# 64 instead of 32 tokens scored by gathers and dots, in a fused attention and expert block

## The reference

```python
def peer(h, w_query, sub_keys, expert_u, expert_v):
    qry = (h @ w_query).reshape(B, S, PEER_HEADS, 2, PEER_HALF)      # 8 heads
    sc = jnp.einsum('bshpd,hpnd->bshpn', qry, sub_keys)              # 2 x 128 key scores
    top_s, top_i = lax.top_k(sc, K)                                  # K = 16
    cand = top_s[..., 0, :, None] + top_s[..., 1, None, :]
    best, flat = lax.top_k(cand.reshape(B, S, PEER_HEADS, K * K), K)
    i1 = flat // K
    i2 = flat % K
    experts = (jnp.take_along_axis(top_i[..., 0, :], i1, axis=-1) * PEER_NKEYS
               + jnp.take_along_axis(top_i[..., 1, :], i2, axis=-1)) # of 16384
    g = jax.nn.softmax(best.astype(jnp.float32), axis=-1).astype(h.dtype)
    ...
    act = jax.nn.gelu(jnp.einsum('td,tkd->tk', xt, u), approximate=False) * gt
    return jnp.einsum('tk,tkd->td', act, expert_v[et])
```

## Time and profile before

| what | value |
| --- | --- |
| median of 3 runs | 1690.3 us (1689.53 to 1692.21) |
| the profiled execution, its time | 1693.6 us |
| its span | 1691.7 us |
| PE busy | 1639.4 us, 97% |
| DVE busy | 1370.9 us, 81% |
| ACT, POOL busy | 773.5 us, 782.3 us (46% each) |
| DMA | 432.17 MB, 255 GB/s on the mean |

### The profile page before, as it was taken

The page is one execution under the profiler, slowest core; times in us unless marked ns, Lnnn a source line. Parts: engine busy times, 40 slices in busy tenths (PEclk is TensorE's granted clock), DMA queues, the critical chain, the costliest instruction groups (busy, mean ns, idle before and its releaser), DMA issues.

```text
span 1691.7 us, 24231 instructions
## 1 busy us (share of the span) xinstructions
PE 1639.4 (97%) x8700; PEld 1440.1 (85%) x8700; DVE 1370.9 (81%) x2691; ACT 773.5 (46%) x1327; POOL 782.3 (46%) x441
## 2 busy tenths in 40 slices
PE   6999999999999999999999899999999999999998
PEld 4687877878799999899999889999999978888886
DVE  7457656676688787999999589888879999888887
ACT  3356546543553444576767333333333343333334
POOL 0322222325356665666666355555545654333331
PEclk9999999999999999999999999999999999999999
DMA  8322242334043432668888999999998999999992
GB/s 338 110 100 87 105 181 89 137 124 150 27 142 121 151 129 97 209 235 350 329 334 339 357 390 374 343 367 353 348 363 322 347 400 398 398 367 376 379 357 98
DMA packets 141676, 432.17 MB, mean 255 GB/s; under 512 B 13584, under 2 KB 58640, under 8 KB 135696
## 3 DMA queue, kind: packets, MB, share of 16 engines
q1 hardware_dynamic: 88592, 265.61, 42.6%
q0 software_dynamic: 41472, 151.01, 23.8%
q10 hardware_dynamic: 11520, 14.42, 2.3%
HBM read 389.31 MB, written 41.68 MB: 255 GB/s over the span
## 4 chain that ended last, share of the span: by engine, by line
PE 66%; DVE 25%; DMA 4%; issue 3%; POOL 1%; ACT 1%; SPq 0%; DVEq 0%; ACTq 0%
PE bank L990 29%; PE bank L934 11%; PE bank L709 10%; PE bank L873 4%; DVE rows L1625 4%; DVE hot_j L1751 3%; DVE hot_i L1743 3%; DMA u_raw<-euT 2%; DVE hot_j L1746 2%; PE bank L735 1%; DVE arena L1703 1%; PE bank L796 1%; DVE slots L1636 1%; DVE arena L1661 1%; DVE arena L1653 1%
## 5 line engine op out<-in xcount | busy, mean ns | idle before, releaser
L934 PE MATMUL bank<-h_split,u_split 128*128 128x352 f32 x3072 | 518.3, 325 | 8.8 <-DVE u_split L1619 7.1
L934 PEld LDWEIGHTS bank<-h_split,u_split 128*128 128x128 f32 x3072 | 496.6, 189 | 16.7 <-DVE u_split L1619 8.2
L990 PE MATMUL bank<-v_late,a_late 128*128 128x512 f32 x1440 | 326.7, 389 | 1.6 <-DVE a_late L1797 1.6
L990 PEld LDWEIGHTS bank<-v_late,a_late 128*128 128x128 f32 x1440 | 270.2, 188 | 57.9 <-issue 1.8
L609 POOL DMA_INDIRECT rows<-ev,idx x128 | 175.5, 1371 | 220.8 <-DVE row_sum L1734 194.7
L582 POOL TENSOR_TENSOR block_split<-arena,block_split 128x1024 fp32r<-128x1024 f32 x48 | 118.1, 2465 | 304.7 <-ACT block_split L1054 304.7
L609 POOL DMA_INDIRECT rows<-eu,idx x128 | 187.6, 1466 | 149.6 <-DVE dots L1625 125.1
L592 POOL TENSOR_TENSOR u_split<-u_raw,u_split 128x1024 fp32r<-128x1024 f32 x72 | 173.8, 2417 | 169.7 <-ACT u_split L1199 169.5
L990 PE MATMUL bank<-v_split,a_split 128*128 128x512 f32 x864 | 205.4, 392 | 2.2 <-DVE a_split L1797 2.2
L990 PEld LDWEIGHTS bank<-v_split,a_split 128*128 128x128 f32 x864 | 162.1, 189 | 33.1 <-issue 2.5
L1734 DVE SCALAR_TENSOR_TENSOR row_sum<-rows,agate,row_sum 128x1024 f32<-128x1024 f32 x127 | 162.7, 1281 | 5.7 <-DMA rows<-ev,idx 1.6
(11 more groups left out here) (283 smaller groups left out, 2521.5 us busy)
## 6 DMA issues: line engine op xcount, KB each, us to landing
u_raw<-euT SPq DMA_DIRECT2D x128, 512.0 KB, 8.4
v_raw<-ev SPq DMA_DIRECT2D x128, 512.0 KB, 7.2
arena<-w_blocks SPq DMA_DIRECT2D x50, 512.0 KB, 9.2
arena<-w_ada SPq DMA_DIRECT2D x12, 2048.0 KB, 8.4
gates_scratch<-stage SPq DMA_DIRECT2D x24, 1024.0 KB, 13.6
gates<-gates_scratch SPq DMA_DIRECT2D x32, 768.0 KB, 10.7
gelu_scratch<-gelus ACTq DMA_DIRECT2D x80, 176.0 KB, 3.7
gelus<-gelu_scratch SPq DMA_DIRECT2D x80, 176.0 KB, 9.1
```

The costliest lines, as they stand in the source:

```text
L934: last = pe.matmul(ps[6 + b][:, 0:TE], us[:, b, wp, k * P:(k + 1) * P], hs[:, xp, k, 0:TE], start=(k == 0 and q == 0), stop=(k == DC - 1 a ...
L990: last = pe.matmul(ps[2 * t + f][:], a[:, ap, t * P:(t + 1) * P], v[:, vp, f * 512:(f + 1) * 512], start=(first and q == 0), stop=True, sk ...
```

## The change

E becomes 64: PE's scores have 320 columns, and there are 64 gathers and dots for these tokens instead of 32 (each gather has 64 tokens in two copies, eight experts of a head in each copy). Their indices are made head by head (`more_index`), so that the first 18 gathers and dots can stand in the ranking: three gathers at the end of POOL's part for heads 1 to 6, three dots ahead of DVE's ranking of heads 2 to 7. The chunks beside the one-hots become 48 with two groups each, where there were 36 with eight groups to three chunks; EARLY goes from 37 to 39, BEFORE from 7 to 5, STASHED from 80 to 92, so that NF goes from 48 to 36. DVE's three splits ahead of the one-hots go to POOL. On SP the last gate stores are spread between u loads, ahead of them stand four v loads, and the gate loads begin with the piece that is needed first. The dots and row sums of the last tile are dealt out anew over the steps.

```diff
--- before.py
+++ after.py
@@ -28,28 +28,32 @@
 RING = 4
 ND = 3
 TD = ND * P
-E = 32
+E = 64
 TE = TD - E
-NE = P * E // P
+NE = E
+COPIES = P // E
+PER_COPY = TOPK // COPIES
 PER_HEAD = 4
 POOL_U = PER_HEAD * HEADS + 4
-EARLY = POOL_U + 1
+EARLY = POOL_U + 3
 GROUPS = TD // 4
-BESIDE = 3 * GROUPS // 8
-BEFORE = 7
+BESIDE = GROUPS // 2
+BEFORE = 5
 STASHED = EARLY + BESIDE + BEFORE
 LATE = 4
 PIECES = 4
 GT = 3
 NF = NK - STASHED
 NG = 5
-MORE_DOTS = 16
-LAST_DOTS = 4
+DOTS_HEAD = 3
+DOTS_RANK = DOTS_HEAD * (HEADS - 2)
+MORE_DOTS = 28
+LAST_DOTS = 7
 DOTS_G = MORE_DOTS + LAST_DOTS
-DOTS_BY = 36
-ACC_FROM = 37
-ACC_F = 38
-E_DOTS, E_GELU, E_GATES, E_TURN = 26, 27, 28, 30
+DOTS_BY = 32
+ACC_FROM = 33
+ACC_F = 10
+E_DOTS, E_GELU, E_GATES, E_TURN = 32, 33, 34, 36
 SPREAD_BANK = (3, 6)
 TURN_BANK = (4, 2, 4, 4, 4)
 FREE = 1
@@ -155,7 +159,7 @@
 def dots_beside(s):
 
     if s <= E_DOTS:
-        return NE * s // E_DOTS
+        return DOTS_RANK + (NE - DOTS_RANK) * s // E_DOTS
     return NE + MORE_DOTS * (s - E_DOTS) // (BESIDE - E_DOTS)
 
 
@@ -169,8 +173,7 @@
 def groups_after(c):
 
     k = c - EARLY
-    first = 8 * (k // 3) + 3 * (k % 3)
-    return range(first, first + (3, 3, 2)[k % 3])
+    return range(2 * k, 2 * k + 2)
 
 
 def value_chunk(v):
@@ -334,6 +337,7 @@
         row_b, whole = (ps[4][:, TT * TOPK * f:TT * TOPK * (f + 1)] for f in range(2))
         first_values = ps[5][:, 0:TT * TOPK].rearrange("p (t k) -> p t k", t=TT)
         den = ps[5][:, TT * TOPK:TT * TOPK + 2 * TT]
+        more_low = ps[5][:, 128:128 + TOPK]
         edge = carve(2, TT * TOPK)
         bijf = carve(2, TT * TOPK)
         pick = carve(2, TT * TOPK, TOPK)
@@ -365,7 +369,7 @@
         vt = carve(RING, D, name="v_raw")
         vs = carve(2, 2, D, split="v_split")
         gt = [nc.alloc_sbuf_tensor_at(f"gates{b}", [P, 4 * TD], F32, offset=at)[:].rearrange("p (n i t) -> p n i t", n=GROUPS // 16, i=4)
-              for b, at in enumerate((arena_at + 4 * top[0], arena_at + 4 * skt_at, hot_at))]
+              for b, at in enumerate((arena_at + 4 * skt_at, hot_at, arena_at + 4 * top[0]))]
         top[0] += 4 * TD
         wgt = carve(2, TD, name="weights")
         ar = carve(2, 2, TD, split="a_split")
@@ -506,22 +510,6 @@
             for c in range(PER_HEAD * HEADS + RING, EARLY + RING):
                 u_load(c)
 
-            for n in range(GROUPS // 16):
-                if n == 0:
-                    for k in range(6):
-                        u_load(EARLY + RING + k)
-                for b in range(4):
-                    sp.wait_ge(staged[b], 4 * (n + 1) + FREE)
-                for k in range(PIECES):
-                    i0 = k * NK // PIECES
-                    sp.dma_start(gates_dram[n][:, i0:i0 + NK // PIECES, :],
-                                 stages[n % 2][:, i0:i0 + NK // PIECES, :]).then_inc(g_out[n % 2], 16)
-                    u_load(EARLY + RING + 6 * (n + 1) + k)
-                for k in range(PIECES, 6):
-                    u_load(EARLY + RING + 6 * (n + 1) + k)
-            for c in range(EARLY + RING + BESIDE + 6, STASHED + RING):
-                u_load(c)
-
             def v_load(i):
 
                 if i >= RING:
@@ -540,15 +528,40 @@
                 sp.wait_ge(w_ready, i - RING + 1)
                 sp.dma_start(gel[:, i % RING, 0:TE], gelu_dram[value_chunk(i)]).then_inc(gl_in[i % RING], 16)
 
-            for n in range(2):
-                sp.wait_ge(g_out[n], 16 * PIECES * GROUPS // 32)
-            v_load(0)
-            gate_load(0)
-            v_load(1)
-            gate_load(1)
-            for i in range(2, RING):
+            def gates_store(n, k, done):
+
+                i0 = k * NK // PIECES
+                sp.dma_start(gates_dram[n][:, i0:i0 + NK // PIECES, :], stages[n % 2][:, i0:i0 + NK // PIECES, :]).then_inc(done, 16)
+
+            LAST = GROUPS // 16 - 1
+            U = BESIDE // (GROUPS // 16)
+            for k in range(U):
+                u_load(EARLY + RING + k)
+            for n in range(LAST):
+                for b in range(4):
+                    sp.wait_ge(staged[b], 4 * (n + 1) + FREE)
+                for k in range(U):
+                    if k < PIECES:
+                        gates_store(n, k, g_out[n % 2])
+                    u_load(EARLY + RING + U * (n + 1) + k)
+            sp.wait_ge(g_out[0], 16 * PIECES * 3)
+            for i in range(RING):
                 v_load(i)
-            gate_load(2)
+            for b in range(4):
+                sp.wait_ge(staged[b], 4 * (LAST + 1) + FREE)
+            first = STASHED // (NK // PIECES)
+            gates_store(LAST, first, g_out[0])
+            u_load(EARLY + RING + BESIDE)
+            for j in range(1, PIECES):
+                gates_store(LAST, (first + j) % PIECES, g_out[1])
+                u_load(EARLY + RING + BESIDE + j)
+            sp.wait_ge(g_out[0], 16 * (PIECES * 3 + 1))
+            for i in range(GT):
+                if i == 1:
+                    sp.wait_ge(g_out[1], 16 * (PIECES * 3 - 1))
+                gate_load(i)
+                if EARLY + RING + BESIDE + PIECES + i < STASHED + RING:
+                    u_load(EARLY + RING + BESIDE + PIECES + i)
             for e in range(RING):
                 sp.wait_ge(gelu_out[e], 16 * STASHED // RING)
             for i in range(NK):
@@ -602,7 +615,10 @@
 
                 if g == 0:
                     pool.wait_ge(turned, 2 * (TT + 1) + 3)
-                    pool.wait_ge(idx_ready, 2)
+                if g < NE and g % PER_COPY == 0:
+                    pool.wait_ge(idx_ready, g // PER_COPY + 1)
+                if g == NE:
+                    pool.wait_ge(idx_ready, HEADS + 1)
                 if g >= NG:
                     pool.wait_ge(rows_used, g - NG + 1)
                 at = idxE[:, g:g + 1] if g < NE else idx[:, (g - NE) % P:(g - NE) % P + 1]
@@ -625,14 +641,18 @@
                     query_low(n + 2)
                 u_low(PER_HEAD * n + 4)
                 u_low(PER_HEAD * n + 5)
-            for c in range(PER_HEAD * HEADS + 2, POOL_U):
+                if 0 < n < HEADS - 1:
+                    for k in range(DOTS_HEAD):
+                        gather(DOTS_HEAD * (n - 1) + k)
+            for c in range(PER_HEAD * HEADS + 2, EARLY):
                 u_low(c)
             for c in range(2):
                 index_pick(HEADS - 1, c)
-
-            for g in range(NG):
+            for c in range(EARLY, EARLY + 2):
+                u_low(c)
+
+            for g in range(DOTS_RANK, DOTS_RANK + NG):
                 gather(g)
-            pool.wait_ge(u_split, EARLY + 2)
             for k in range(BESIDE):
                 u_low(EARLY + 2 + k)
                 for g in range(NG + dots_beside(max(0, k - 1)), NG + dots_beside(k)):
@@ -1286,11 +1306,11 @@
                 gelu(c)
                 u_high(c + 2)
                 gelu_stash(c)
-                if c == PER_HEAD * HEADS + 1:
+                if c == EARLY - 3:
                     best_gates(HEADS - 1)
 
             sa.wait_ge(slotsT_done, 3)
-            sa.wait_ge(idx_ready, 2)
+            sa.wait_ge(idx_ready, HEADS + 1)
             for f in range(3):
                 act_(slotsT[:, f, :], ps[f][:, 0:TD], ACT.Copy).then_inc(slotsT_ready, 1)
             sa.wait_ge(slotsT_ready, 1)
@@ -1322,8 +1342,9 @@
                         hot_gates(g + 3)
                 if c == EARLY + E_GELU:
                     sa.wait_ge(rows_used, NE)
-                    for q in range(P // E):
-                        last = act_(agate[TE - 2 * P:P, q * E:(q + 1) * E], dotsE[q * E:(q + 1) * E, :], ACT.Gelu)
+                    to = agate[TE - 2 * P:P, :].rearrange("p (n q r) -> p n q r", n=HEADS, q=COPIES)
+                    for q in range(COPIES):
+                        last = act_(to[:, :, q, :], dotsE[q * E:(q + 1) * E, :].rearrange("p (n r) -> p n r", n=HEADS), ACT.Gelu)
                     last.then_inc(dots_gelu, 1)
                 if c == EARLY + E_TURN:
                     sa.wait_ge(slotsT_done, 4)
@@ -1642,7 +1663,21 @@
                 nv.scalar_tensor_tensor(idx[:], slots[:, 0, TT - 1, :], float(NK), slots[:, 1, TT - 1, :],
                                         ALU.mult, ALU.add).then_inc(idx_ready, 1)
 
+            def more_index(i):
+
+                ve.wait_ge(pick_summed, 2 * i + 2 + FREE)
+                of, at = slice(TE - 2 * P, P), i * TOPK
+                step(nv.tensor_copy(more_low[of, :], slots[of, 1, ND - 1, at:at + TOPK]))
+                for q in range(COPIES):
+                    k = q * PER_COPY
+                    ins = nv.scalar_tensor_tensor(idxE[q * E:(q + 1) * E, i * PER_COPY:(i + 1) * PER_COPY], slots[of, 0, ND - 1, at + k:at + k + PER_COPY],
+                                                  float(NK), more_low[of, k:k + PER_COPY], ALU.mult, ALU.add)
+                ins.then_inc(idx_ready, 1)
+
             def rank(i, finish_before=False):
+                if i >= 2:
+                    for k in range(DOTS_HEAD):
```

(12 more changed lines are left out.)

## The result

The changed kernel took 1710.85 us, the median of 4 runs (1706.3 to 1712.97), against 1691.26 (1689.53 to 1696.13) for the kernel before: a ratio of 1.0108, 95% interval 1.0091 to 1.0126. The forecast was 1685.0 us with a range of 1662 to 1699. It is slower, where the forecast had it 0.3% faster, and it lies above the range.

A forecast was written before the change was run, and what follows sets the result against it. It took PE, busy 97% of the span, as the bound: ranking +28, one-hots +34.4, change-over -10.0, values -57.5 give -5.1 on 1691.7, so 1686.6; less 1.4 for the median, about 1685 us, range 1662 to 1699.

The forecast's parts named there:

- The change-over: From the one-hots to the first values: seven chunks instead of nine, 31.2 us instead of 41.2, so -10.0 us.
- the wait: In the stage before the first values: waits for u rows beside gate stores and loads, kept at 6.4 us (bounds 0 and 12).
- The ranking: Stage before the one-hots: dots on DVE lengthen a head from 28.5 to 34.0 us; +28 us, bounds about +1 and +36.
- Strict turns: In the ranking: DVE and POOL alternate by whole instructions, so three dots take 10.5 us; throughout with a cast wait, +36.
- Head 2: Second head of the ranking to get a number: its start was forecast 1.1 us later than before.
- the tail: End of the ranking, up to the first one-hot: it loses a DVE split, -1 us.
- The one-hots: Stage with 48 chunks for 36: PE's count plus 2% and slow clock, 264 us against 229.6, +34.4 us.
- the rival let DVE decide: One-hot stage: DVE bounds it from 1.48 us a dot; at 1.77 the stage takes 277, time 1698; chance 0.15.
- The values: From the first values on: PE has 12 score chunks less and 35 shorter ones, -57.5 us.
- the rival in which DMA bounds it: Late values: at only 375 GB/s a step takes 4.23 us, +14, time 1699; chance 0.10.
- Cheap dots: Ranking: dots slip in with few holds; one hold a head gives +5 and 1662, two +17 and 1674; chance 0.27.

The follow-up runs named there:

- e5: e2 with the seven last-tile dots that lay in the change-over moved into the value steps: 1668.63 us, 0.9874 of the kernel before.
- e9: The changed kernel, ranking dots left in place, with only the seven dots ahead of the first values moved into the value steps: 1697.06 us.
- e2: The changed kernel with each head's three ranking dots moved from the top of the ranking to just ahead of the multiplies POOL's picks wait for: 1675.81 us.
- e8: The changed kernel with each of the 18 ranking dots replaced, in its place, by a sum of the gathered row alone: 1681.78 us.

## Why the prediction was wrong, point by point

**The change-over is the step that failed.** It read "the bytes to be moved before the first values are about the same per chunk, so I leave the wait at 6.4": -10.0 us, and it was +1.7. The four gate stores of 1 MB, the three gate loads of 768 KB and the value rows belong to the stage and not to its chunks, and the gathers ahead grew. It could have been seen beforehand: the earlier trace rows have the DMA share of that stage at 1.02 with 392 GB/s, so little time could come out of it without bytes coming out, and the question was how many of the 16.16 MB go with the two chunks. The upper bound taken for the wait, 12 us, gave 36.8 us; PE's rest in the stage was 15.1. e5 and e9 show the cause by taking 8.7 and 9.0 us out with the gathers alone: 6.6 and 6.8 of it is the gate load's shorter way, the other 2.2 that it is issued earlier.

**The ranking: right mechanism, short by 9.1 us.** It cost 37.15 us where the upper bound was 36. Strict turns, DVE becoming the bound, 34.0 us a head: measured 33.9 to 34.1 from head 3 on, and 171.4 us over the five steps for 170.5 (the first was 35.3 for 31.9, the second 33.9 for 36.6). What the sum had too small are the two ends. Head 2 started 6.1 us later than before (533.02 for 526.92) and not 1.1: its three rows had not landed, DVE stood 3.74 us, and the first dots were held as well. A gather takes about 8.1 us to land at that point, and in the plan its rows were always there. At the tail, after the last head's MAX8 at 704.43, the way to the first one-hot is 38.8 us for 36.65 before, where -1 was forecast: the splits given to POOL hold DVE's cast, its last pair of multiplies and a copy behind them. The timeline of DVE after:

```profile
723.58 2.26 DVE L1724 CAST arena<-arena 128x128 f32<-128x128 uint32 x1
...
727.74 4.43 DVE L1739 TENSOR_TENSOR arena<-arena,cst 128x1024 f32<-128x1024 f32 x2
...
739.04 2.40 DVE L1749 COPY gate_more<-slots 128x128 f32<-128x128 f32 x1
```

In the last head of before the first two took 1.54 and 2.36 us and the same copy 0.22, 5.0 less together; picks that are held less and DVE's own splits, which are gone, give part of that back. POOL's splits were issued at 723.36 and 727.55, each just ahead of the first two, and two more ran from 736.67 to 741.35, over the copy. The rows beforehand had this price for a dot and a split; it was not applied to the splits that the change itself adds to POOL there.

**The one-hots: right.** 262.1 us for 264. PE's chunk with two groups is 5.30 us over the first 32 chunks (3.52 and 1.78). The dots there took 1.54 us each (110.66 us for 72), which is past the 1.48 at which the rival let DVE decide, and PE still set the pace: DVE's stage was not simply the sum of its busy times, since part of a held dot's time is given up where DVE is ahead.

**The values: right.** -59.6 for -57.5. The late stage has PE busy 374.57 of 374.60 us, at 370 GB/s on the mean, so the rival in which DMA bounds it is refuted; DVE had 30 us over in it. The pitch at 320 columns is 146.7 ns (3.52 us a chunk) for the forecast's 147.7.

**Cheap dots**, the rival at 0.27, didn't happen in after, since they stood where POOL's queue is full; in e2 they did, with no hold at all.

**Why slower and not faster.** PE's score chunk did become 0.34 us shorter, 43.5 us over 128. The kernel after loses it in two places that have nothing to do with the columns: 37 us in the ranking, of which e2 gives back 32.2 by taking the dots out of the turns, and a stage with full DMA engines, of which e5 gives back 8.7. With both undone the same 64 tokens make the kernel 1.3% faster than before (e5, ratio 0.9874 [0.9857, 0.9890]).

**Open.** The runs of after lie 1706 to 1713 us and the profiled one is the quickest; what adds up to 7 us in the others no trace here shows. PE's waits for one-hots grow by 4 us in e2 (11.3 us for 7.3 in after) and are 7.7 us in e5; whether that is the change or the execution that happened to be profiled was not followed up. Which property of a dot makes POOL hold it is open too, as said at e8.

## What to carry to other kernels

Ask of each DVE instruction that is to fill a gap whether a trace shows its kind held by POOL (here multiplies, splits and dots with two operands, but casts and copies with one as well; sums were not), and whether POOL's queue is busy in that gap. If both hold, it can cost a whole POOL instruction each time, and moving it some 3 us, ahead of the instruction that releases POOL, can make it free. For a stage whose DMA share is 1, count its bytes by kind, what belongs to the stage and what to a chunk: here taking two chunks out left the time as it was. A rearrangement of several stages is best tried one place at a time: here two badly chosen places hid a gain of 1.3%.

## What the runs showed of the hardware

- Two engines that both have such work queued alternate instruction by instruction, in both directions: dots of 1.15 us came out at 3.36 to 3.39, picks and splits of 2.40 at 3.28 to 3.36 (after, 557 to 602 us). A cast of 0.22 us came out at 1.77 (before), a copy of 0.22 at 2.40 (after). The waits stand in no idle time, only in longer durations.
- A long wait was paid twice on PE: after 4.98 us a chunk took 5.79 us instead of 3.52, at a granted clock of 0.61; after 9.95 us 18 value matmuls took 6.60 instead of 4.11, at 0.64; in before, after 2.25 us, 5.96, at 0.71. The two levels of the clock are 1.2 and 2.4 GHz. In e5, after a wait of 2.12 us, the same 18 took 4.36 at a granted clock of 1.00. The Trainium skill, TensorE: Matmul & The Clock Gate, Part 1: The HAM clock gate, has the engine at half rate after it was idle; the rows at 0.61, 0.64 and 0.71 agree.
- All 16 DMA engines together gave 404 to 409 GB/s over 34 to 43 us of mixed stores, loads and gathers, in after, e2, e5 and e9 alike.
- A gather of 128 rows of 4 KB landed 8.1 us after its issue ahead of head 2 (the median over the 18 of the ranking is 5.8) and 12.5 us in the change-over, where the DMA engines were full.
